# A result tile brought by SyncE's plain copy and added by GpSimd, in place of an adding load by GpSimd's queue (both layers)

## The reference, cut to what matters

```python
    for e in range(N_EXPERTS):
        hid = jax.nn.silu(xf @ w_gate_l[e]) * (xf @ w_up_l[e])
        y = y + combine[:, e:e + 1] * (hid @ w_down_l[e]).astype(jnp.float32)
    ...
        h = layer_norm(ALPHA * h + moe_ffn(h, router_w, router_b, w_gate_l[l], w_up_l[l], w_down_l[l]), ln2_g[l], ln2_b[l])
```

## Time and profile before

| | us |
|---|---|
| three runs | 982.09, 979.58, 982.34; median 982.09 |
| the profiled execution, its own time | 981.18 |
| its span | 979.3 |
| busy in the span: PE, DVE, ACT, POOL | 947.1 (97%), 820.7 (84%), 656.8 (67%), 260.5 (27%) |
| granted TensorE clock, mean | 0.992 |

### The profile page before, as it was taken

The page is one execution under the profiler, slowest core; times in us unless marked ns, Lnnn a source line. Parts: engine busy times, 40 slices in busy tenths (PEclk is TensorE's granted clock), DMA queues, the critical chain, the costliest instruction groups (busy, mean ns, idle before and its releaser), DMA issues. The chain is left out here.

```text
span 979.3 us, 15394 instructions
## 1 busy us (share of the span) xinstructions
PE 947.1 (97%) x5212; PEld 789.2 (81%) x5212; DVE 820.7 (84%) x1205; ACT 656.8 (67%) x941; POOL 260.5 (27%) x343
## 2 busy tenths in 40 slices
PE   6999999999999999999999999999999999999993
PEld 5998867788888888888779997787888888888882
DVE  8967677789999899899876676578998998998996
ACT  5345541378888888888755556317888888888882
POOL 1433343471111111110323334336111111111022
PEclk9999999999999999999999999999999999999997
DMA  9853850599999999998894035439999999999875
GB/s 347 294 170 126 268 200 22 196 351 410 382 370 367 365 363 366 373 369 333 239 284 170 26 133 184 144 117 373 410 389 373 363 376 362 388 358 370 299 208 129
DMA packets 85693, 278.27 MB, mean 284 GB/s; under 512 B 8787, under 2 KB 11083, under 8 KB 85614
## 3 DMA queue, kind: packets, MB, share of 16 engines
q1 hardware_dynamic: 67024, 240.40, 67.3%
q0 software_dynamic: 11040, 21.14, 7.5%
q10 hardware_dynamic: 7566, 15.96, 4.8%
HBM read 266.51 MB, written 30.37 MB: 303 GB/s over the span
## 5 line engine op out<-in xcount | busy, mean ns | idle before, releaser
L1596 DVE TENSOR_TENSOR w_lo<-ring,w_hi 128x1024 fp32r<-128x1024 f32 x256 | 303.1, 1235 | 36.0 <-ACT w_hi L2241 33.6
L2241 ACT ACTIVATE w_hi<-ring 128x1024 fp32r<-128x1024 f32 x256 | 261.2, 1059 | 39.9 <-PE PS L1111 26.7
L1063 PE MATMUL PS<-w_hi,x_hi 128*128 128x512 f32 x512 | 164.1, 401 | 0.0
L1068 PE MATMUL PS<-w_lo,x_hi 128*128 128x512 f32 x512 | 160.6, 394 | 0.0
L1063 PE MATMUL PS<-w_hi,x_lo 128*128 128x512 f32 x512 | 160.0, 393 | 0.0
L1603 DVE TENSOR_TENSOR w_lo<-ring,w_hi 128x1024 fp32r<-128x1024 f32 x128 | 153.7, 1220 | 4.4 <-ACT w_hi L2254 4.4
L2254 ACT ACTIVATE w_hi<-ring 128x1024 fp32r<-128x1024 f32 x128 | 135.6, 1061 | 29.6 <-PE PS L1068 27.9
L2608 POOL DMA_INDIRECT M<-xs,idx x30 | 56.0, 1867 | 232.7 <-PE PS L1042 204.1
L1063 PEld LDWEIGHTS PS<-w_hi,x_lo 128*128 128x128 f32 x512 | 96.3, 188 | 23.3
L1068 PEld LDWEIGHTS PS<-w_lo,x_hi 128*128 128x128 f32 x512 | 96.3, 188 | 22.1
L1063 PEld LDWEIGHTS PS<-w_hi,x_hi 128*128 128x128 f32 x512 | 94.1, 189 | 19.6
(11 more groups left out here) (293 smaller groups left out, 1619.5 us busy)
## 6 DMA issues: line engine op xcount, KB each, us to landing
ring<-in_w_gate SPq DMA_DIRECT2D x32, 2048.0 KB, 15.0
ring<-in_w_down SPq DMA_DIRECT2D x32, 2048.0 KB, 15.3
ring<-in_w_up SPq DMA_DIRECT2D x32, 2048.0 KB, 17.2
ring<-in_w_in SPq DMA_DIRECT2D x8, 2048.0 KB, 17.7
ring<-in_w_out SPq DMA_DIRECT2D x4, 2048.0 KB, 8.6
ys<-H SPq DMA_DIRECT2D x2, 3072.0 KB, 20.0
H<-ys POOLq DMA_DIRECT2D x12, 512.0 KB, 8.5
M<-in_cache_k ACTq DMA_DIRECT2D x8, 512.0 KB, 3.7
```

The source lines that it names most:

```text
L1063: pe.matmul(PS[:, n, :], x[:, c:c + P], w_hi[j][:, k * 512:(k + 1) * 512], start=(j == 0 and k == 0 and x is x_hi[par]), stop=False)
L1068: mm = pe.matmul(PS[:, n, :], x_hi[par][:, c:c + P], lo[:, k * 512:(k + 1) * 512], start=False, stop=(j == 3 and k == 1))
L1596: dve.tensor_tensor(lo, w, w_hi[j][:, :].bitcast(F32), ALU.subtract).then_inc(up_lo, 1)
L2241: act.activation(w_hi[j][:, :], quarter(3 * par + n, j)[0], ACT.Copy).then_inc(up_hi, 1)
```

## The change

In both layers the second result rows (k=1) of tile 2 are no longer brought by an adding DMA of POOL's queue. When the scatters have landed, POOL raises a new semaphore `first_closed`; SP waits for it behind its loop over the experts and copies these 128 rows by a plain DMA into `second`, the first 1024 columns of the buffer `FT`, which is free then. POOL issues the adding DMAs of k=0 for the other tiles, waits for the copy, adds `second` to tile 2 of `H` with a tensor operation, and goes on with k=1 for the other tiles; the one adding DMA of tile 2 that is left (k=0) waits for the addition. The counts of `y_in[2]` are halved.

```diff
@@ (buffers and semaphores)
+        second = FT[:, :, :].rearrange("p k n -> p (k n)")[:, 0:D]
...
+        first_closed, second_in, second_added = sem("first_closed"), sem("second_in"), sem("second_added")
@@ (SP)
-                        sp.wait_ge(y_in[j], 32 * l)
+                        sp.wait_ge(y_in[j], (16 if j == 2 else 32) * l)
...
                 round_(l, 16 * rb, True)
+                sp.wait_ge(first_closed, l + 1)
+                sp.dma_start(second, result_rows(l, 1, 2)).then_inc(second_in, 16)
                 sp.wait_ge(routed, l + 1)
@@ (DVE, sum_added)
-                dve.wait_ge(y_in[j], 32 * (l + 1))
+                dve.wait_ge(y_in[j], (16 if j == 2 else 32) * (l + 1))
@@ (POOL)
             def results_added(l):
 
                 pool.wait_ge(h_scaled, l + 1)
-                for k in range(2):
-                    for j in order(LN2[l]):
-                        if k == 1:
-                            pool.wait_ge(y_in[j], 32 * l + 16)
-                        pool.dma_start(H[0:TN[j], j, :], result_rows(l, k, j), accum_op=ALU.add).then_inc(y_in[j], 16)
+                for j in order(LN2[l]):
+                    if j != 2:
+                        pool.dma_start(H[0:TN[j], j, :], result_rows(l, 0, j), accum_op=ALU.add).then_inc(y_in[j], 16)
+                pool.wait_ge(second_in, 16 * (l + 1))
+                pool.tensor_tensor(H[:, 2, :], H[:, 2, :], second, ALU.add).then_inc(second_added, 1)
+                for j in order(LN2[l]):
+                    if j == 2:
+                        pool.wait_ge(second_added, l + 1)
+                    else:
+                        pool.wait_ge(y_in[j], 32 * l + 16)
+                    pool.dma_start(H[0:TN[j], j, :], result_rows(l, 0 if j == 2 else 1, j), accum_op=ALU.add
+                                   ).then_inc(y_in[j], 16)
...
                 pool.sem_inc(round_closed, 1)
                 if first:
+                    pool.sem_inc(first_closed, 1)
                     results_added(l)
```

More of the change, by code:

```diff
@@ L2730, in _ @@
                     for j in tiles_of(l):
-                        pool.wait_ge(y_in[j], 32 * (l + 1))
+                        pool.wait_ge(y_in[j], (16 if j == 2 else 32) * (l + 1))
                     pool.dma_start(ys[l][0:768, :].rearrange("(a p) n -> p a n", p=64),
```

## The result

| | before | changed |
|---|---|---|
| median | 981.89 us (979.58 to 982.34, 4 runs) | 1013.17 us (1011.04 to 1016.33, 4 runs) |
| ratio | | 1.033, 95% interval 1.0312 to 1.0349 |
| profiled execution, its own time | 981.18 | 1011.04 |
| its span | 979.3 | 1009.1 |
| TensorE busy | 947.1 (97%) | 955.6 (95%) |

The change costs 31.3 us by the medians and 29.9 by the profiled executions. The forecast was 1021.5 (1003 to 1036): right in sign and mechanism, 8.3 us too high. Part of that nearness is luck: three terms were off by more than the sum shows, as the last sections tell.

What follows compares the result with a forecast made beforehand. TensorE was taken to bound the kernel (97% busy) except at the layer ends, where adding DMAs and then expert 15's late down load decide. Layer 0 +23.5 and layer 1 +15.9 on 981.18 gave 1020.6, plus 0.9: 1021.5 us (1003 to 1036).

Steps and rivals of the forecast that it cites:

- Rival 4: Both layer ends: the down load isn't late and only the adding chain counts; -3.2 us, 979; chance 2%.
- The release, 475.7 and 944.0: SP's queue, both layer ends: expert 15's down load can't go before the last scatter lands, 475.7 and 944.0.
- The transfer, layer 0: End of layer 0: copy, `w_in` and down matrix share engines with adding DMAs at 0.133 MB/us; landing 504.0, not 477.3.
- SP's small costs: SP, both layer ends: issues of 0.4 us and the read of the round count vanish behind bytes queued in front.
- The transfer, layer 1: End of layer 1: copy done at 948.4, down matrix 15.8 us later, landing at 965.4 instead of 941.8.
- Rival 1: Both layer ends: SP's queue at 0.40 MB/us, unhindered by adding DMAs; +14.0 us together, 996; chance 12%.
- rival 2: Both layer ends: queues share time equally; landings 2.2 and 6.0 us earlier, 1013; within the forecast, no separate chance.
- From landing to first sum, 12.6: Both layer ends, from expert 15's down landing: 12.1 us of work up to the first sum, plus 0.5 for low clock.
- Rival 3: Both layer ends: TensorE's clock stays at the low level up to the sums; +19 us, 1040; chance 11%.
- Given back, 1.2 and 2.0: Ends of layers 0 and 1: DVE's sum no longer waits for the adding DMA; -1.2 and -2.0 us.
- GpSimd's addition, 2.7: POOL, each layer end: adding `second` to tile 2 of `H` costs 2.7 us, hidden.
- this layer's 23.5: Layer 0's net loss: first sum 24.7 us later, less the 1.2 us wait that falls away, +23.5.

Runs made afterwards that it cites:

- the five traces: Layer 1 of the changed kernel and four variants (last layer only, no GpSimd addition, two with filler matmuls); 16.5 to 19.9 us from SP's copy to ACT's start.
- The bridged kernel: Changed kernel with 80 (layer 0) and 22 (layer 1) identity matmuls put into TensorE's wait for the last down pieces; 1011.13 us, ratio 1.0315.
- the kernel with too many fillers: Changed kernel with 150 (layer 0) and 50 (layer 1) identity matmuls ahead of expert 15's down matmuls; 1024.32 us, ratio 1.0429.

## Why the prediction was right, point by point

- **The mechanism.** Shown: the down load of expert 15 waits in SP's order for the scatters, ACT and TensorE wait for it (the chain, the waits), the wait alone gives the loss, and moving the same instructions behind the load removes it. Rival 4, not slower, fell. Right in the forecast was also that fewer adding DMAs can give 3.2 us at most; no run showed any of it in its median.
- **The release, 475.7 and 944.0.** This is the term that was mis-sized: "the last scatter ... lands at 475.7 and 944.0" took the landing of 7.8 and 7.2 us from a kernel in which the 2 MB down load and the norm rows go out just before the scatter; q1 has 90 to 94% of the DMA engines' time until it lands. In the changed kernel they are themselves held back, q1 moves nothing in that stretch, and the scatter lands in 3.1 and 2.6. SP's copy goes at 471.06, and in layer 1 at 963.32, or 939.5 in the time of before (less the 23.8 of layer 0): 4.6 and 4.5 us before the forecast. The run with the copy behind the loads brings 7.9 and 7.1 us back, and the wait alone, without any copy, has 3.1 and 2.6: that shows the cause.
- **The transfer, layer 0.** From release to landing I had 28.3 us (475.7 to 504.0); it took 29.6. The two errors against each other leave the landing at 500.7, 3.3 us early.
- **SP's small costs.** "Vanish behind the bytes queued in front" did not hold in layer 1. The down load goes out 1.67 us after the copy (963.32 and 964.99), the copy's 0.52 MB are through before its data come, and the queues at 967 show one queue alone:

```profile
q0 software_dynamic: 50, 0.20, 103.0%
```

  The load's data begin at about 968.8, 5.5 us after the release, where the forecast had 4.4. In the kernel without any adding DMA q1 drops to 0.09 MB in the microsecond of 952 as well, between copy and load, and this layer takes 12.3 us where 1.7, 6.6 and 1.2 make 9.5.
- **The transfer, layer 1.** Here I had 21.4 (944.0 to 965.4), and it took 16.4. With the release that makes the landing 9.5 us early, which is the whole difference between 15.9 and 6.2 in this layer. As told above, about 1 to 3.4 us of it are this one execution's; the five traces took 16.5 to 19.9. Queues per microsecond (packets, MB, share), at 973 and at 975:

```profile
q0 software_dynamic: 32, 0.13, 65.4%
q1 hardware_dynamic: 34, 0.14, 36.8%
...
q1 hardware_dynamic: 91, 0.37, 91.3%
q0 software_dynamic: 15, 0.02, 12.8%
```

  Where both queues have work, it is one packet for one, as taken from the earlier trace rows, and an adding packet costs the engines about twice as much: 65.4% for 32 against 36.8% for 34. q1 gets 0.14 MB/us, as forecast (0.133). Rival 1, q1 at 0.40 beside q0, and rival 2, equal time, are both wrong in such a microsecond. That rival 2's 1013 is the measured time is chance. The Trainium skill ("DMA: Bandwidth & Descriptors", section "Queues, rings and completion order") has each engine go round its queues packet by packet; the trace agrees with like counts, 32 and 34, of packets that are one row of 4 KB each.

  But q0 did not have work all the time, as my 15.8 us assumed. A tile's second adding DMA is issued only when its first has landed, and q0 runs dry between the two series: in 969 to 971 and 975 to 977, where q1 goes at 0.27 to 0.41 MB/us. Over 965 to 979, q1 moved 2.58 MB and q0 1.37. All five traces with two DMAs of 128 rows in the first series have two or three microseconds of 0.29 or more for q1 in the second of these pauses, the one without GpSimd's addition too. The wait alone has three in the first series and only one microsecond in which q1 is above 0.18 (971, with 0.27); q1 moved 2.22 MB and q0 2.06 from 965 until ACT began at 983.6. That it is the number in flight which makes the pause fits all six; no run varies it by itself. Nor does the mean rate set the landing alone: in the five, q1 had moved 2.8 to 3.5 MB when the load had landed, of which the copy and the load are 2.6, so part of the norm rows was through before the last piece of the load.
- **Packet sizes, layer 0.** The queues at 480:

```profile
q0 software_dynamic: 40, 0.16, 81.8%
q1 hardware_dynamic: 41, 0.08, 25.1%
```

  Again one for one, but the packets of `w_in` (rows of 512 elements) are half as large: q1 gets 0.08 MB/us there and not 0.133. That eats what the pauses give (0.54 MB in 482 to 484), and would explain why this layer's transfer came out near the forecast; no run tells the two apart.
- **From landing to first sum, 12.6.** Measured 13.0 and 12.4. In layer 0 two errors met: without the low clock it is 11.2 and not 12.1, and the low clock costs 1.8 and not 0.5, so it was not "mostly hidden" behind DVE's quarters. Rival 3, half clock up to the sums at 19 us, is wrong: TensorE works at the low level for 5.3 us in layer 0 and about 4 in layer 1. The row that was held against it, matmuls at the kernel's start, is no good witness for the length: the single matmuls there take 0.42 us until 7.9 and 0.28 from then on, so slow ones for 2.7 us and not 3.7, and the granted clock reads 1.00 throughout.
- **Given back, 1.2 and 2.0.** Right: both waits are gone.
- **GpSimd's addition, 2.7.** It took 5.6 and 5.8, twice the size, and was hidden as forecast. Over half of it is waiting for VectorE, as the last section shows.
- **Not forecast: 3.3 us between the layers.** From the third sum of layer 0 to the last scatter of layer 1 it is 439.0 us before and 442.3 after, with the clock at 0.57 in 532 to 536 and 0.63 in 700 to 704 while TensorE is busy. The bridged kernel has neither, and 438.9. That the idle stretch causes them is not shown: the kernel with too many fillers had no such stretch and still a fall (0.72 at 548 to 552, 441.1 us), and five others had one fall each at other places, with 0.2 to 1.6 us more than 439.0 in this stretch. That this layer's 23.5 looks as good as measured (20.5 + 3.3 = 23.8) is luck: the term was 3.0 too high and the 3.3 had no term.

The sum as measured: 20.5 + 3.3 + 6.2 = 30.0 by the third sums, 29.9 by the executions' own times, against 23.5 + 15.9 = 39.4.

## What to carry to other kernels

An instruction with a wait, put into an in-order DMA queue, is priced by what stands behind it: find the next bulk load there, and the time at which it is needed, before anything else; the adding DMA saved was worth 3 us at most, and the place of the wait for it cost 30. When a change holds back a load, don't take latencies of other transfers from a trace in which that load ran beside them. In a shared stretch count packets, not bytes, look at each queue's packet size and kind, and ask when the other queue runs dry. And take the same stretch from several traces before explaining 2 us of it.

## What the runs showed of the hardware

- A scatter of the software queue landed 2.6 to 3.1 us after its issue with the hardware queue empty, and 7.1 to 7.9 with a 2 MB load and 1 MB of norm rows in it (q1 at 88 to 94% of the DMA engines' time).
- GpSimd and VectorE hold each other up. GpSimd's addition of 128x1024 took 5.63 and 5.76 us beside VectorE's two-input operations, 3.1 with the copy behind the loads, 2.4 (layer 1) and 2.7 (layer 0) when it came last. VectorE's timeline in the changed kernel, beside the additions of 474.80 to 480.43 and of 967.22 to 972.98:

```profile
474.69 3.48 DVE L1607 TENSOR_TENSOR w_lo<-ring,w_hi 128x1024 fp32r<-128x1024 f32 x3
478.09 0.67 DVE L1614 TENSOR_TENSOR M<-M,PS 128x512 f32<-128x512 f32 x1
478.69 2.83 DVE L1607 TENSOR_TENSOR w_lo<-ring,w_hi 128x1024 fp32r<-128x1024 f32 x1
...
967.24 3.49 DVE L1607 TENSOR_TENSOR w_lo<-ring,w_hi 128x1024 fp32r<-128x1024 f32 x3
970.65 0.68 DVE L1614 TENSOR_TENSOR M<-M,PS 128x512 f32<-128x512 f32 x1
971.25 2.83 DVE L1607 TENSOR_TENSOR w_lo<-ring,w_hi 128x1024 fp32r<-128x1024 f32 x1
```

  The first three subtractions, with both inputs in SBUF, run at their usual 1.2 us each, though the addition has been issued. From the start of L1614, which has one input in SBUF and one in PSUM, to the end of the addition it is 2.34 and 2.33 us, as long as the addition takes by itself. The fourth subtraction takes 2.83 us and ends 1.1 us after the addition in both layers. So it looks as if the addition waits for all three and the fourth then waits for the addition, one at a time. The Trainium skill ("SBUF — State Buffer", section "Who interferes with whom") says that a VectorE instruction with two inputs in SBUF contends with a GpSimd instruction that reads SBUF; the trace agrees, and it cuts both ways.
- The granted clock fell to 0.57 and 0.63 for some 4 us while TensorE was busy all through (4.00 of 4.00 us in 700 to 704), and at other places in six more of the twelve executions profiled; the kernel before and four others had no such fall between the layers.
